# Two transformer blocks on one core: the first attention's weights turned by VectorE and transfers instead of TensorE

## The reference

```python
a = gelu(z_a); u, v = split(a)                       # spatial gating
y_a = (u * chunked_spatial_gating(layer_norm(v))) @ w_a_out
c = p * sigmoid(g_lin)                               # z_b = p, g_lin
c = causal_depthwise_conv(c, cv_w, cv_b)             # 31 taps, 512 channels
y_b = silu(layer_norm(c)) @ w_b_out
# stick-breaking attention, 8 heads of 64, query blocks of 128 (z_c = q, k, v)
zs = q @ k.T * scale; mask = k_pos < q_pos
log_1m_beta = where(mask, log_sigmoid(-zs), 0)
cs = cumsum(log_1m_beta)
a = where(mask, exp(log_sigmoid(zs) + cs[-1] - cs), 0)
y_c = (a @ v) @ w_c_out
merged = sigmoid(z_g0 + b0) * y_a + sigmoid(z_g1 + b1) * y_b + sigmoid(z_g2 + b2) * y_c
x = x + merged @ w_out                               # then a gated feed-forward part
```

## Time and profile before

| | us |
|---|---|
| median of three runs | 1275.33 |
| profiled execution | 1275.76 |
| its span | 1274.0 |
| TensorE busy | 1263.9 |
| VectorE busy | 869.3 |
| ScalarE busy | 586.3 |
| GpSimd busy | 88.1 |

### The profile page before, as it was taken

One profiled execution on the slowest core, in us unless ns is written; L12 is line 12 of the kernel. 1 busy time (PEld: TensorE's weight loads), 2 busy tenths in 40 slices (PEclk: granted clock), 3 DMA queues, 4 the chain that ended last, 5 costly groups with the idle time before them and its releaser, 6 DMA issues.

```text
span 1274.0 us, 15378 instructions
## 1 busy us (share of the span) xinstructions
PE 1263.9 (99%) x5760; PEld 1016.6 (80%) x5760; DVE 869.3 (68%) x1164; ACT 586.3 (46%) x866; POOL 88.1 (7%) x68
## 2 busy tenths in 40 slices
PE   8999999999999999999999999999999999999998
PEld 7888777888888888888888888888877777777886
DVE  5489899899877776666666333675469998655544
ACT  7235466232263443333333223512368899444223
POOL 0000222000000200000000001300012220000000
PEclk9999999999999999999999999999999999999999
DMA  7556222422322333323322222249825555665421
GB/s 264 178 130 172 66 67 67 165 97 77 120 75 97 99 100 99 99 99 99 98 91 102 90 88 91 99 125 215 239 76 124 140 159 131 183 148 149 161 70 67
DMA packets 220922, 153.36 MB, mean 120 GB/s; under 512 B 119704, under 2 KB 196416, under 8 KB 220608
## 3 DMA queue, kind: packets, MB, share of 16 engines
q1 hardware_dynamic: 220272, 151.53, 40.7%
q10 hardware_dynamic: 592, 1.05, 0.2%
HBM read 134.21 MB, written 18.35 MB: 120 GB/s over the span
## 4 chain that ended last, share of the span: by engine, by line
PE 97%; DVE 1%; DMA 1%; ACT 0%; SPq 0%; issue 0%; ACTq 0%
PE PS L1903 97%; PE PS L1970 1%; DMA STAGE<-in_w_in 1%; DVE WL L1163 0%; DVE XL L1201 0%; DVE XG L1193 0%; ACT XH L744 0%; ACT WH L716 0%; DVE TB L1752 0%; DVE XT L1896 0%; ACT SQF L1133 0%; DVE XT L1891 0%; DVE BLR L1790 0%; SPq L521 0%; SPq L520 0%
## 5 line engine op out<-in xcount | busy, mean ns | idle before, releaser
L716 ACT ACTIVATE WH<-STAGE 128x1024 fp32r<-128x1024 f32 x214 | 225.9, 1058 | 540.2 <-PE PS L1903 528.6
L1903 PE MATMUL PS<-XH,WH 128*128 128x512 f32 x960 | 380.9, 397 | 0.0
L1163 DVE TENSOR_TENSOR WL<-STAGE,WH 128x1024 fp32r<-128x1024 f32 x214 | 275.4, 1289 | 147.8 <-ACT WH L716 147.4
L1903 PE MATMUL PS<-XH,WL 128*128 128x512 f32 x960 | 373.9, 389 | 0.0
L1903 PE MATMUL PS<-XL,WH 128*128 128x512 f32 x960 | 373.8, 389 | 0.0
L1903 PEld LDWEIGHTS PS<-XH,WH 128*128 128x128 f32 x960 | 180.2, 188 | 43.5 <-issue 5.5
L1903 PEld LDWEIGHTS PS<-XL,WH 128*128 128x128 f32 x960 | 180.3, 188 | 39.0 <-issue 2.6
L1903 PEld LDWEIGHTS PS<-XH,WL 128*128 128x128 f32 x960 | 180.2, 188 | 38.1
L1903 PE MATMUL PS<-WH,XH 128*128 128x512 f32 x224 | 88.1, 393 | 0.6 <-DVE WL L1163 0.6
L1903 PE MATMUL PS<-WH,XL 128*128 128x512 f32 x224 | 87.2, 389 | 0.0
L1903 PE MATMUL PS<-WL,XH 128*128 128x512 f32 x224 | 87.2, 389 | 0.0
(11 more groups left out here) (289 smaller groups left out, 1782.3 us busy)
## 6 DMA issues: line engine op xcount, KB each, us to landing
STAGE<-in_w_in SPq DMA_DIRECT2D x51, 1024.0 KB, 5.2
STAGE<-in_w_up SPq DMA_DIRECT2D x22, 1024.0 KB, 5.1
STAGE<-in_w_down SPq DMA_DIRECT2D x11, 1024.0 KB, 5.0
probabilities<-TB SPq DMA_DIRECT2D x48, 128.0 KB, 5.8
PT<-probabilities SPq DMA_DIRECT2D x18, 256.0 KB, 5.6
STAGE<-in_w_out SPq DMA_DIRECT2D x4, 1024.0 KB, 5.3
STAGE<-in_w_rnn_out SPq DMA_DIRECT2D x4, 1024.0 KB, 5.3
STAGE<-in_w_attn_out SPq DMA_DIRECT2D x4, 1024.0 KB, 5.3
```

The source lines that it names most:

```text
L716: act.activation(ring(WH, n), staged(n), ACT.Copy).then_inc(hi_done, 1)
L1163: dve.tensor_tensor(ring(WL, n), staged(n), ring(WH, n).bitcast(F32), ALU.subtract)\
L1903: return pe.matmul(out_, lhsT, rhs, start=start, stop=stop, skip_group_check=True)
```

## The change

The turn of each step no longer goes through TensorE and ScalarE. VectorE transposes 32x32 blocks of BT into a new buffer BTT (three places: over SS and SQ, over the second half of ATT, and for step 11 over BT0), four transfers store it into a new tensor in memory, AROW, so that whole 128x128 blocks are turned, and eight transfers per pair load AT from it. Stores and loads stand in SyncE's loop. The values matmuls move from passes 6, 9, 12 and behind gate unit 3 to passes 8, 11, 14 and 17. Fourteen taps move from passes 4 to 11 to the gate units. GpSimd clears SS after its last step instead of before the first, since BTT lies over it. Some semaphores are merged.

```diff
+        BTT = [at("BTT0", [P, 1024], F32, 91), at("BTT1", [P, 1024], F32, 175), at("BTT2", [P, 1024], F32, 100)]
+        AROW = [nc.dram_tensor(f"attention_rows{i}", [1024, P], F32, kind="Internal").ap()
+                for i in range(12)]
+        def pair_tile(s):
+            return BTT[2 if s == 11 else s % 2][:, 0:2 * STEP_W[s % 3]]
@@ SyncE @@
+            def at_store(s):
+                sp.wait_ge(at_t, s + 1)
+                for a in range(4):
+                    sp.dma_start(AROW[s][0:2 * STEP_W[s % 3]].rearrange("(b i) (a j) -> a i b j", i=32, j=32)[a],
+                                 pair_tile(s)[32 * a:32 * a + 32].rearrange("p (b j) -> p b j", j=32))\
+                      .then_inc(at_out[s % 2], 16)
+            def at_load(p):
+                sp.wait_ge(at_out[0], 64 * ((3 * p + 2) // 2 + 1))
+                sp.wait_ge(at_out[1], 64 * ((3 * p + 1) // 2 + 1))
+                if p:
+                    sp.wait_ge(av_done, p)
+                for s in range(3 * p, 3 * p + 3):
+                    w = STEP_W[s % 3]
+                    for par in range(2):
+                        rows_ = AROW[s][par * w:(par + 1) * w].rearrange("(k p) c -> p k c", p=P)
...
+                            sp.dma_start(AT[:, par, 512:640], rows_[:, 2]).then_inc(at_ready, 16)
...
+                step = p - U_B // 2 - 5
+                if 0 <= step < 7:
+                    for s in ((0,), (1, 2), (3, 4), (5, 6), (7, 8), (9, 10), (11,))[step]:
+                        at_store(s)
+                    if step in (1, 3, 4, 6):
+                        at_load((1, 3, 4, 6).index(step))
@@ GpSimd @@
-            pool.wait_ge(rb_done, 1)
-            pool.memset(SS[:], 0.0).then_inc(ss_clear, 1)
...
+            pool.wait_ge(at_out[0], 64 * 6)
+            pool.memset(SS[:], 0.0).then_inc(ss_clear, 1)
@@ ScalarE @@
-            def pair_turned(s):
...
             def pair_out(p):
                 act.wait_ge(av_done, p + 1)
+                if p == 2:
+                    act.wait_ge(at_out[1], 64 * 5)
...
-                if i >= 6 and i % 3 == 0:
-                    pair_out(i // 3 - 2)
-                if 3 <= i < 15:
-                    pair_turned(i - 3)
+                if i >= 8 and i % 3 == 2:
+                    pair_out((i - 8) // 3)
@@ VectorE @@
+            def pair_turn(s):
+                w = STEP_W[s % 3]
+                dve.wait_ge(a_ready, s + 1)
+                if 2 <= s < 11:
+                    dve.wait_ge(at_out[s % 2], 64 * (s // 2))
+                dve.transpose(pair_tile(s).rearrange("p (a c) -> p a c", c=w), BT[s % 2][:, :, 0:w])\
+                   .then_inc(at_t, 1)
...
                     pair_mask(i - 1)
+                if i >= 3:
+                    pair_turn(i - 3)
                 lo(U_B + i + 4)
...
-                    taps(3 if i < 6 else 4)
+                    taps(2)
...
+                        if b == 0 and q == 0 and r < 3:
+                            pair_turn(9 + r)
...
+                            if b == 0 and q == 0:
+                                dve.wait_ge(at_out[0], 64 * 6)
+                                dve.wait_ge(at_out[1], 64 * 6)
...
-                        taps((4, 4, 4, 4, 6, 3)[r])
+                        taps((5, 5, 5, 5, 5, 3)[r])
@@ TensorE @@
-            def pair_turn(s):
...
             def pair_values(p):
-                pe.wait_ge(at_ready, 4 * p + 4)
+                pe.wait_ge(at_ready, 128 * p + 128)
...
-                if i >= 6 and i % 3 == 0:
-                    pair_values(i // 3 - 2)
-                if 3 <= i < 15:
-                    pair_turn(i - 3)
+                if i >= 8 and i % 3 == 2:
+                    pair_values((i - 8) // 3)
...
+                            if b == 0 and r == 2:
+                                pe.wait_ge(att_read, 4)
...
+                    if b == 0 and q == 0:
+                        stick_pe(17)
```

More of the change, by code:

```diff
@@ L310, in program @@
                                                   sem("sc_scan"))
+        at_out = [sem("at_out0"), sem("at_out1")]
         a_ready, at_t, at_ready, av_done, att_read = (sem("a_ready"), sem("at_t"), sem("at_ready"),
@@ L314, in program @@
         tg_act, tg_used = sem("tg_act"), sem("tg_used")
-        c_sum, c_mean, c_cent, c_sq, c_ssum, c_var, c_ve, c_sd, c_norm, c_ready = (
-            sem("c_sum"), sem("c_mean"), sem("c_cent"), sem("c_sq"), sem("c_ssum"), sem("c_var"),
+        c_sum, c_mean, c_cent, c_sq, c_ve, c_sd, c_norm, c_ready = (
+            sem("c_sum"), sem("c_mean"), sem("c_cent"), sem("c_sq"),
             sem("c_ve"), sem("c_sd"), sem("c_norm"), sem("c_ready"))
@@ L493, in p_load @@
                       .then_inc(pt_in, 16)
+            def at_store(s):
[13 more added lines that the diff above has]
+                        rows_ = AROW[s][par * w:(par + 1) * w].rearrange("(k p) c -> p k c", p=P)
+                        if s % 3 == 0:
+                            sp.dma_start(AT[:, par, 0:256].rearrange("p (k c) -> p k c", c=P), rows_[:, 0:2])\
+                              .then_inc(at_ready, 16)
+                            sp.dma_start(AT[:, par, 512:640], rows_[:, 2]).then_inc(at_ready, 16)
+                        elif s % 3 == 1:
+                            sp.dma_start(AT[:, par, 0:1152].rearrange("p (k c) -> p k c", c=384)[:, :, 256:384],
+                                         rows_).then_inc(at_ready, 16)
+                        else:
+                            sp.dma_start(AT[:, par, 384:1920].rearrange("p (k c) -> p k c", c=384)[:, :, 0:P],
+                                         rows_).then_inc(at_ready, 16)
             def q2_load(h):
@@ L865, in _ @@
                         hi(n + 4)
-                        if b == 0 and q == 0 and r < 4:
+                        if b == 0 and q == 0:
                             stick_act(12 + r)
@@ L1482, in _ @@
                         dve.wait_ge(av_done, 4)
-                        dve.wait_ge(at_ready, 16)
                     dve.tensor_tensor((GS, GSB)[p // 4][:, p % 4, :], PS[:, p % 4, :], RBC[:], ALU.mult)\
@@ L1503, in _ @@
                     dve.wait_ge(c_sq, 4)
-                    dve.tensor_tensor(TG0[:], TG0[:], UU[:, 3, :], ALU.add).then_inc(c_ssum, 1)
+                    dve.tensor_tensor(TG0[:], TG0[:], UU[:, 3, :], ALU.add).then_inc(c_sum, 1)
                 if p == 4:
-                    dve.wait_ge(c_var, 1)
+                    dve.wait_ge(c_mean, 2)
                     dve.tensor_scalar(TG0[:], PS[:, 5, :], 1.0 / W, EPS, ALU.mult, ALU.add)\
@@ L2140, in gates_first @@
                     if p == 4:
-                        pe.wait_ge(c_ssum, 1)
-                        mm(PS[:, 5, :], ONES[:], TG0[:], True, True).then_inc(c_var, 1)
+                        pe.wait_ge(c_sum, 2)
+                        mm(PS[:, 5, :], ONES[:], TG0[:], True, True).then_inc(c_mean, 1)
                 pe.wait_ge(c_cent, KW)
```

## The result

The changed kernel takes **1299.92 us** (median of 4 runs, 1298.78 to 1300.08) against 1275.27 before (1275.14 to 1275.87, 4 runs): ratio 1.019, interval 1.0173 to 1.0208. I had forecast 1284.7, between 1273 and 1292. The direction was right. The size was not: +24.6 us measured, +9.4 forecast. The span grew from 1274.0 to 1298.3, and these 24.3 us are what has to be accounted for.

The account below looks back on a forecast made before the run. TensorE, busy 99% of the span, was taken as the bound: -8.4 for transposes removed, +6.8 and +11.0 for waits on pairs 1 and 3, +9.4 in sum, gave 1284.7 us, eight in ten between 1273 and 1292.

Parts of the forecast that it names:

- The 80 transposes: TensorE's turning transposes in the first attention: eight turns of six and four of eight, removed, save 8.4 us.
- Transfer 19: STAGE transfer ahead of pair 3's stores and load: issued behind low part 35, 28.9 us after gate unit 0 ends.
- The moved taps: Fourteen VectorE taps of 0.68 us moved to the gate units: 9.5 us less in the first stage, costed at nothing.
- Values 1 and 3: Values matmuls of pairs 1 and 3 on TensorE: wait for the load of AT, 6.8 and 11.0 us.
- 384 KB +5.9: Store of 384 KB in 128-byte runs behind a STAGE transfer: landed 5.9 us after that transfer is issued.
- The passes 6, 8, 10: VectorE passes in the first stage waiting for earlier steps' stores: 1.5 us late in pass 6, about 2.6 by pass 9.
- inside the same 6.8: Scores held back 1 to 2 us by VectorE's store waits: counted within pair 1's 6.8 us wait, nothing added.
- transfer 16: STAGE transfer ahead of pair 1's load, behind low part 29: issued at 176.6 us, weights landed 15.0 us later.
- the term without a row: Load of 1280 KB of weights into AT: 6.7 us, bounds 5.0 and 9, plus 0.9 still in the rings.
- rival C: TensorE's clock falls to half behind both weight waits, about 1.5 us each: 1288 us; chance 0.25.
- D: Rival: waits for stores make VectorE set the pace, with late turns and low parts: beyond 1290, to 1296; chance 0.09.

Follow-up runs that it names:

- places for every step: The changed kernel with eight places instead of three for VectorE's turned blocks and a semaphore per step, SyncE's queue order kept: 1296.77 us, ratio 1.0165.
- both: The changed kernel with eight buffer places, every second step's stores and the loads of pairs 1 and 3 one transfer earlier: 1275.28 us, ratio 0.9999.

## Why the prediction was wrong

**What was right.** TensorE sets the end, each of its waits costs its time. The 80 transposes are worth 8.4: the account closes to 0.3 us with it. Transfer 19 goes out 28.8 us after the end of gate unit 0 (209.45 to 238.21), forecast 28.9. VectorE's block transposes take 0.97 and 1.23 us (forecast 0.96 and 1.24). The moved taps are free in the kernel before. Values 1 and 3 wait for the load, values 0 and 2 do not; for values 0 that was luck, since it waits 2.95 us as soon as TensorE isn't held at the scores ("places for every step").

**Where it failed: the price of the stores, the scores' waits and the clock.** "384 KB +5.9" was a line through two stores of the earlier trace rows (512 KB +7.0, 1024 KB +11.4). Measured is +9.15. Both rows of before were of an otherwise similar queue, a STAGE transfer and then stores, so the line looked safe. Yet the row did not even hold for its own size: the 512 KB of step 11 have landed only when the load goes out at +8.25 (238.21 to 246.46). In before the four issues behind the transfer of 941.09 take 3.38 us, here they take 5.21 (238.64 to 243.85):

```profile
941.50 3.38 SPq L477 DMA_DIRECT2D probabilities<-TB  x4
```

The bytes show the order, in the rate of the DMA engines of after between 236 and 256 us in slices of 0.5 us:

```profile
GB/s 0 0 0 0 0 0 41 49 180 393 397 397 377 325 214 218 209 178 162 6 0 0 4 196 196 197 196 183 290 313 179 251 256 232 238 271 250 291 332 401
```

From 240.5 to 243 the transfer flows at 325 to 397 GB/s; the store's half megabyte follows at 162 to 218; some 2 us of nearly nothing; then the load. The three barely overlap, so a short store behind a transfer pays for the whole transfer. The line had 2.6 us for a store of no size, and that is too little for such a constant. How much of the +9.15 of step 1 comes from the stores of step 2 issued right behind it, no run shows. The Trainium skill (DMA: Bandwidth & Descriptors, Specifications) wants at least 512 bytes in a piece for full rate; the store's 128-byte pieces at 162 to 218 GB/s against up to 397 for the transfer agree.

**What hangs on it.** (1) The passes 6, 8, 10: I had VectorE late by 1.5 us in pass 6 and the scores held "inside the same 6.8". VectorE waited 4.8, 3.5 and 4.5 us, the scores 9.8 in sum. (2) By that transfer 16 went out at 181.7, not 176.6, since it follows low part 29 in VectorE's order. (3) Chains of 17.4 and 16.15 us instead of 15.0 and 13.7. The load itself, the term without a row, was taken well for pair 1: from the issue of its first part to landing 199.14 - 191.53 = 7.6, forecast 6.7 + 0.9 = 7.6; for pair 3 it is 254.36 - 246.46 = 7.9, forecast 6.7, half of that chain's miss. The waits for weights came to 2.0 and 10.2 (forecast 6.8 and 11.0): the first is small only because TensorE had lost its time at the scores, and the second is near only because it had lost 3.5 at ATT. Without the buffers' waits ("places for every step") they are 2.95, 6.91 and 13.87.

**What was not in the sum.** ATT: the copy of pair 2's output overwrites the buffer of step 9, whose store is issued behind transfer 18. I did not name this wait; 3.5 us. I had asked what waits for the buffers among VectorE's instructions only. "Places for every step" takes it away, and the wait of values 3 grows by 3.8 (10.04 to 13.87), so its own price is nearly nil, and it belongs to the chain like the rest. The clock: 0 in the sum, 3 us in rival C. It was up to 5.8 by experiment. C had the mechanism at two waits, and it came at three places, because the scores waited as well.

**By terms.** Forecast -8.4 + 6.8 + 11.0 = +9.4. Measured, -8.4, weights 12.2, scores 9.8, ATT 3.5, clock 6.8. In the forecast's own terms: what TensorE waits up to values 1 is 9.8 + 2.0 = 11.8 instead of 6.8 (scores "inside the same 6.8" failed), from there to values 3 it is 3.5 + 10.2 = 13.7 instead of 11.0, and the clock is 6.8 instead of 0: +5.0, +2.7 and +6.8. The clock, put at nothing, is the largest miss. Rivals C and D were both true, and I had priced each alone: C's clock over the forecast's waits, D's VectorE without the clock. Together they end beyond either.

## What to carry to other kernels

A result that leaves an engine through a DMA queue shared with large prefetches pays for the prefetch ahead of it: before the work is moved there, write down each queue's order, and put the short store ahead of the long transfer. Here the stores of every second step and two of the loads, queued one transfer earlier, took 22 us off, and half of the stores ahead of the transfer, with fewer taps in three units, another 6; buffers alone took off 3. And where the engine that sets the end is never idle, price each new wait with the clock behind it: in the change it added up to 5.8 us to 25.5 of waits.

## What the runs showed that I had not expected

The clock falls after the work has begun again: behind the 2.67 us before 158.28 the matmuls start at the full rate and run at 0.50 from 160 to 163 us; in the wait of 10 us it had fallen before the wait was over (249 to 254). In after it did not fall behind a wait of 1.46 us. In "both" it did not fall behind one of 1.72 at 228, and it did behind one of 1.88 at 205 (stretch of "both"):

```profile
207.00:211.00 4.00, 3.98 (x16) 1.58 (x16) 4.00 (x5) 1.67 (x2) 0.00 (x0) 0.57 0.22 36
```

Taking work from the engine that sets the end gave less than that work where another chain was just covered: 68 transposes, 7.3 us, brought 2.0.

What stays open: why four issues of a store behind STAGE take 4.8 to 6.8 us here and 3.4 in before; and why the kernels with early stores spread over 3 to 5 us from run to run where before spreads over 1.3. The clock, which fell behind some short waits and not behind others, could do that, but no run tests it.
